# Decode rows of the row-wise projections: one pass of matmuls behind the second half of the contraction, instead of one pass behind each half

## The reference

```python
# GLA (layers 0 and 3): v has 1024 columns
q, k, v, g, a = _split(h @ w_in, [GLA_KEY_DIM, GLA_KEY_DIM, GLA_VAL_DIM, GLA_VAL_DIM, GLA_GATE_RANK])
# DSA (layer 1): k has 1024 columns; it is also an output (k_rows_prompt, k_rows_sample)
q, k, v, g, iq, ik, iw = _split(h @ w_in, [DSA_WIDTH] * 4 + [IDX_HEADS * IDX_DIM, IDX_DIM, IDX_HEADS])
```

## Time and profile before

| | us |
|---|---|
| median of 3 runs | 1150.73 |
| lowest and highest run | 1149.67 and 1153.07 |
| span of the profiled execution | 1153.2 |

### The profile page before, as it was taken

One profiled execution on the slowest core, in us unless ns is written; L12 is line 12 of the kernel. 1 busy time (PEld: TensorE's weight loads), 2 busy tenths in 40 slices (PEclk: granted clock), 3 DMA queues, 4 the chain that ended last, 5 costly groups with the idle time before them and its releaser, 6 DMA issues. The chain is left out here.

```text
span 1153.2 us, 25599 instructions
## 1 busy us (share of the span) xinstructions
PE 1115.8 (97%) x10579; PEld 976.9 (85%) x10579; DVE 674.4 (58%) x1215; ACT 494.4 (43%) x968; POOL 382.5 (33%) x321
## 2 busy tenths in 40 slices
PE   8999999899999999999999999999999999999897
PEld 6889888799758988888955599999999889888796
DVE  6462255764999779776444555595444362255742
ACT  6542466643443322222254554322453451467643
POOL 5534313234313423114300044353344245312230
PEclk9999999999999999999999999999999999999999
DMA  5235233333314787884779932233220335233202
GB/s 174 96 110 165 87 116 111 129 82 100 112 56 151 237 280 237 273 308 138 256 285 409 377 116 91 66 101 127 83 74 3 111 107 163 78 128 111 97 33 78
DMA packets 127788, 168.81 MB, mean 146 GB/s; under 512 B 20385, under 2 KB 93481, under 8 KB 127664
## 3 DMA queue, kind: packets, MB, share of 16 engines
q1 hardware_dynamic: 115609, 152.59, 39.6%
q10 hardware_dynamic: 12062, 14.59, 3.6%
HBM read 150.70 MB, written 16.81 MB: 145 GB/s over the span
## 5 line engine op out<-in xcount | busy, mean ns | idle before, releaser
L737 POOL TENSOR_TENSOR w_lo<-raw,w_hi 128x512 fp32r<-128x512 f32 (+2 forms) x267 | 359.9, 1380 | 691.4 <-ACT w_hi L1501 691.4
L773 PE MATMUL psum<-h_hi,w_hi 128*128 128x272 f32 x1616 | 471.2, 292 | 6.6 <-DVE h_lo L2425 4.7
L775 PE MATMUL psum<-h_hi,w_lo 128*128 128x272 f32 x1616 | 467.3, 289 | 0.0
L774 PE MATMUL psum<-h_lo,w_hi 128*128 128x272 f32 x1616 | 464.9, 288 | 0.0
L773 PEld LDWEIGHTS psum<-h_hi,w_hi 128*128 128x128 f32 x1616 | 303.3, 188 | 20.2 <-issue 15.3
L774 PEld LDWEIGHTS psum<-h_lo,w_hi 128*128 128x128 f32 x1616 | 303.7, 188 | 0.1
L775 PEld LDWEIGHTS psum<-h_hi,w_lo 128*128 128x128 f32 x1616 | 303.0, 187 | 0.0
L1501 ACT ACTIVATE w_hi<-raw 128x1024 fp32r<-128x1024 f32 (+1 forms) x137 | 135.5, 1034 | 118.5 <-PE psum L775 81.0
L773 PE MATMUL psum<-w_hi,h_hi 128*128 128x512 f32 (+2 forms) x352 | 125.6, 357 | 1.4 <-DVE dsa_score_s L2519 0.8
L775 PE MATMUL psum<-w_hi,h_lo 128*128 128x512 f32 (+2 forms) x352 | 122.5, 348 | 2.3 <-issue 2.3
L774 PE MATMUL psum<-w_lo,h_hi 128*128 128x512 f32 (+2 forms) x352 | 122.5, 348 | 0.7 <-issue 0.7
(11 more groups left out here) (331 smaller groups left out, 1367.3 us busy)
## 6 DMA issues: line engine op xcount, KB each, us to landing
smp_keys<-in_cache_k_dram SPq DMA_DIRECT2D x128, 256.0 KB, 4.7
raw<-in_gla_w_in_dram SPq DMA_DIRECT2D x23, 1024.0 KB, 5.3
raw<-in_dsa_w_in_dram SPq DMA_DIRECT2D x17, 1024.0 KB, 5.3
spare<-in_cache_v_dram SPq DMA_DIRECT2D x34, 512.0 KB, 8.3
raw<-in_cache_v_dram SPq DMA_DIRECT2D x30, 512.0 KB, 8.6
gla_s_in<-in_state_gla_dram SPq DMA_DIRECT2D x16, 512.0 KB, 7.8
raw<-in_gla_w_out_dram SPq DMA_DIRECT2D x8, 1024.0 KB, 6.7
out_dram<-gla_s_in ACTq DMA_DIRECT2D x16, 512.0 KB, 4.6
```

What stands on the lines that cost most here:

```text
L737: pool.tensor_tensor(copies(key, pair_view(w_lo, key)[:, k]), raw_copies(key, k), copies(key, pair_view(w_hi, key)[:, k].bitcast(F32)), AL ...
L773: pe.matmul(out, lh, rh, start=start, stop=False)
L774: pe.matmul(out, lh, rl, start=False, stop=False)
L775: return pe.matmul(out, ll, rh, start=False, stop=stop)
```

## The change

The decode rows leave the loop over the halves. The prompt tiles run through both halves first; then the decode tile claims its bank and runs all eight channel tiles in one go, the first four from the raw buffer of the first half and the last four from that of the second. The signal `("item", key)` is now raised by the last prompt tile of a half, and a new signal `("raw", key)`, for both halves, by the last decode matmul. SyncE's loads into these buffers wait for the new signal, and so would GpSimd's use of a raw buffer at L709. Matmuls, operands and their number stay.

```diff
@@ SyncE, -550,7 @@
                     elif s < RAW and by_rows(old):
-                        sp.wait_ge(*on("proj", ("item", old)))
+                        sp.wait_ge(*on("proj", ("raw", old)))
@@ GpSimd, -706,7 @@
                         if by_rows(bands_after):
-                            pool.wait_ge(*on("proj", ("item", bands_after)))
+                            pool.wait_ge(*on("proj", ("raw", bands_after)))
@@ t_job, -888,20 +888,12 @@
-                    for t in range(TILES):
+                    for t in range(NP_T):
                         if before_tile:
                             before_tile(x, t)
                         if x == 0:
                             bs.append(claim(next_bank(banks), ("proj", name, t), (reader_name, name, t)))
                         for k in range(kk):
-                            if t == SMP:
-                                if k0 + k == 0:
-                                    pe.wait_ge(*(on("h_s", name[0]) if name[0] else on("h_s", 0, SMP, 0)))
-                                for j in range(4):
-                                    mm = pe.matmul(psum[band(j), bs[t], 0:P], h_s[:, k0 + k, :],
-                                                   raw_view(key)[:, k, j * P:(j + 1) * P],
-                                                   start=k0 + k == 0, stop=k0 + k == KT - 1)
-                                continue
                             if t == 0:
                                 split_in(key, k)
@@ -909,12 +901,23 @@
-                        last_t = ((("item", key),),) if t == TILES - 1 else ()
+                        last_t = ((("item", key),),) if t == NP_T - 1 else ()
                         if x == len(keys) - 1:
                             mm.then_inc(*sig("proj", (name, t), also=last_t))
-                        elif t == TILES - 1:
+                        elif t == NP_T - 1:
                             mm.then_inc(*sig("proj", ("item", key)))
+                    if before_tile:
+                        before_tile(x, SMP)
                     k0 += kk
+
+                b = claim(next_bank(banks), ("proj", name, SMP), (reader_name, name, SMP))
+                pe.wait_ge(*(on("h_s", name[0]) if name[0] else on("h_s", 0, SMP, 0)))
+                for k in range(KT):
+                    w = raw_view(keys[k // 4])[:, k % 4]
+                    for j in range(4):
+                        mm = pe.matmul(psum[band(j), b, 0:P], h_s[:, k, :], w[:, j * P:(j + 1) * P],
+                                       start=k == 0, stop=k == KT - 1)
+                mm.then_inc(*sig("proj", (name, SMP), also=tuple((("raw", key),) for key in keys)))
```

## The result

The changed kernel takes 1154.58 us (median of 20 runs, 1151.32 to 1157.33) where the kernel before, run beside it, takes 1152.22 (20 runs, 1149.67 to 1155.03). The ratio is 1.0023, with a 95% interval of 1.0013 to 1.0033: 2.6 us slower (0.0023 x 1152.22; the medians are 2.4 us apart), less than 0.3% but clear of the scatter. The forecast of 1151.2 us was 0.5 us above the median then shown; the sign of its sum was right, the size was not, and the measured time lies just above the range (1154.4).

A forecast was written before the change was run, and what follows sets the result against it. The tensor engine, busy 97% of 1153.2 us, was taken as the bound. Merging -2.3, key block 0 stall +2.3, last layer's value block 1 +0.5 gave +0.5 us on the 1150.73 median: 1151.2 us, range 1148.4 to 1154.4.

The forecast's parts named there:

- The gain from merging: Decode passes (L901), 12 merged into 6: six entries and exits of 0.38 us go, 2.3 us gained (1.9 at least).
- The stop: Sparse layer, behind key block 0: late load holds ScalarE, tensor engine waits for third old-key tile, 2.3 us (1.7 to 2.6).
- rival B: Clock falls behind the new idle stretch in key block 0, costing 1.7 us: 1152.9 us; chance 0.20.
- Value blocks 1: Late low halves stall the tensor engine: last layer 0.5 us (0.4 to 1.3), first layer nothing if the clock falls again.
- What I costed at nothing: Late loads behind sparse key block 1, page loads and gated layers' k 1: hidden; otherwise 1 to 2 us a place.
- The sum: Whole kernel: -2.3 + 2.3 + 0.5 + 0, a difference of +0.5 us, giving 1151.2 us; ends -0.2 to +2.0.
- C: Key block 0's load lands after 7.9 us: stall 4.7 us plus a clock drop of 1.7, 1155.3 us; chance 0.12.
- A: Late loads are hidden after all, including ScalarE's stop in key block 0: 1148.4 us; chance 0.12.
- D: Merged passes save nothing, entering and leaving costs as much per half as before; only losses stay: 1153.5 us; chance 0.08.

The follow-up runs named there:

- changed, again: The changed kernel repeated unchanged, beside two other runs on one chip: 1153.41 us, ratio 1.0019 to the kernel before.
- held buffers only: The kernel before with its twelve passes, only the release of both raw buffers moved to the end of the block: 1155.82 us, ratio 1.0043.
- no stores: The changed kernel without ScalarE's five stores of block 0's key rows in the sparse layer and the wait for them: 1153.66 us, ratio 1.0012.
- q 0 held back: The changed kernel with SyncE's load of q 0 held until key block 1's first half is done: 1153.45 us, ratio 1.0013.
- the one with the split moved: The changed kernel with ScalarE's split of key block 1's second half behind all eight old-key tiles: 1150.73 us, 0.9990; again 1150.79 us, 0.9986.
- the kernel with key block 0 in halves: The changed kernel with the sparse layer's key block 0 alone in its old form, pass and buffer release per half: 1151.18 us, ratio 1.0000.

## Why the prediction was wrong, step by step

The stretch behind key block 0 in all the traces that have the stop, below a first row without it. "Third tile" is the start of its matmul, counted from the end of the block; "stretch" runs to the key transposes.

| kernel | load landed after | third tile | stretch | clock behind it |
|---|---|---|---|---|
| before | early enough | 6.1 | 14.46 | full |
| changed | 6.8 | 9.5 | 20.50 | half |
| changed, again | 5.6 | 8.3 | 16.70 | full |
| held buffers only | 6.4 | 9.1 | 17.47 | full |
| no stores | 5.2 | 7.9 | 17.71 | half, for a shorter time |
| q 0 held back | 5.1 | 7.8 | 16.18 | full |

- **The gain from merging.** 0.38 us a block predicted, 0.34 measured, 2.0 us in place of 2.3. The mechanism was right. The edges went as the sum had it; the 32 records that a pass gained took 1.89 - 1.01 = 0.88 us, where 32 steps of 0.026 are 0.84, and that is the missing 0.04.
- **The stop.** Place, chain and formula held: landing + 0.13 + 0.07 - 3.24 - 0.2 gives 2.4 us for 5.6 and 3.6 for 6.8, and the third tile came 2.2 and 3.4 us late. What was too narrow is the bound on the landing. I took 4.9 to 5.8 us, its lower part from the value blocks of the other layers, and put 7.9 aside as an outlier of one; in the ten traces with the load held back behind key block 0 it took 5.1 to 6.8, 5.7 on average. At 5.7 the stop is 2.5 us, close to the 2.3 of the sum, and up to 3.4 happens.
- **The clock.** This is the step that failed. I had it as rival B with a chance of 0.20 and 1.7 us, and outside the sum. Among the five traces with a stop and nothing to fill it, it fell in two, once behind 3.4 us and once behind 2.15, and not behind 2.95, 2.2 and 1.7. It cost 2.7 us in the first (the two steps of 2.93 and 2.94 in place of 1.61) and 1.5 in the second, so (2.7 + 1.5) / 5 = 0.8 us on average of the five. The ratios leave some more: from the changed kernel (1.0023 and 1.0019) to the one with the split moved (0.9990 and 0.9986) it is 0.0033, 3.8 us, and less the 2.5 of the stop 1.3 us. Both are estimates: the first rests on five executions, the second on ratios whose intervals reach about 0.001 to either side. How often the clock falls behind the stop stays open. The mean granted clocks fit but do not decide: the changed kernel has 0.9948, the kernel before on the three chips used behind it 0.9961 to 0.9968, but side by side on one chip they are 0.9957 and 0.9961, and the kernel with key block 0 in halves, which has no stop, has 0.9958. The price of a fall was sized from the first layer, 4 us at 0.66 and 0.50; the half clock lasted longer in the profiled execution.
- **Value blocks 1.** Last layer: 0.5 us predicted. From the block's start to the fifth slice it took 3.50 us (921.38 to 924.88) and was 2.88 (a slice of three products is 0.70, four of them and the entry), so 0.6. First layer: nothing predicted, as the clock would fall there again. It stayed up in this execution, and the place took 3.63 us, 0.7 more than at full clock and less than the 4.45 of the profile before, as the text had it. In the fourteen traces the clock fell here in eight, so the 0.7 counts in some executions and not in others.

```profile
919.05 4.99 POOL L737 TENSOR_TENSOR w_lo<-raw,w_hi 128x512 fp32r<-128x512 f32 x4 [15.09 <-ACT w_hi L1504]
921.38 0.50 PE L773 MATMUL psum<-w_hi,h_hi 128*128 128x512 f32 x1
...
924.09 0.50 PE L773 MATMUL psum<-w_hi,h_hi 128*128 128x512 f32 x1 [0.27 <-POOL w_lo L737]
```

- **What I costed at nothing.** It held: behind key block 1 ScalarE was idle 3.92 us on the load of q 1 and began the split at 372.52, GpSimd at 373.66, and no wait of the tensor engine for it shows. No wait for k 1 of the gated layers shows either, and the waits at the page loads are no longer than before (2.0 us in place of 2.3 at the value pages).
- **The sum.** With what was measured: -2.0 for merging, +2.5 for the stop at the average landing, +0.6 and up to +0.7 for the value blocks, +0.8 to +1.3 for the clock, together +1.9 to +3.1 us; the ratio says +2.6. Three small errors went the same way, 0.3 + 0.2 + up to 0.8, and the clock was left out.
- **The rivals.** What happened is B in part of the executions, and most of C in the profiled one: the landing was 6.8 where C has 7.9, the stop 3.4 where it has 4.7, the clock fell. A is out by the stop in every trace of the changed kernel, D by the 1.89 us of the merged pass (it wanted over 2.1).

The price of a clock that falls belonged into the sum as soon as the change made a new idle stretch beside an old one, with the chance as its weight. I gave it a chance, but then let the likeliest single case stand for the whole. My own 0.20 x 1.7 would have added only 0.3 us, so the chance and the price were too low as well.

That the measured 1154.58 lies above the range has a second cause, which is no part of the mechanism. The kernel before was itself measured 1.5 us higher with twenty runs than with the three that were shown, and the end of the range was 3.2 us above the forecast. Of the 3.4 us between forecast and measurement, 1.5 are this base, and 1.9 are what the change cost beyond the 0.5 of the sum; on the base that was shown, the same loss of 2.4 us between the medians would have ended at 1153.1, inside the range.

The Trainium skill, "TensorE: Matmul & The Clock Gate", section "What's actually happening", has the moment at which the clock changes vary from run to run of one and the same kernel. The two profiled executions of the changed kernel agree: half clock behind the stop in one, full clock in the other.

## What to carry to other kernels

When a buffer is held longer, look for the engine that waits for the late load and then for what stands behind that wait in its program: here the load landed at 323.9 us and the tensor engine came to the first product with it only at 353.8, but the copy behind it was needed at once. Moving the early split behind the urgent copies cost nothing that shows and turned a loss of 0.2% into a gain of about 0.1%, as far as that can be measured. A new idle stretch on the tensor engine has two prices, its length and, in some executions, a slower clock behind it; the second was 2.7 us beside a stop of 3.4 in one execution and nothing in others.

## What the runs showed of the hardware

- A stretch in which the tensor engine stood still for 1.3 to 1.8 us and then, some 3 us later, for 1.7 to 3.4 us was followed by the half clock in two of five traces, for up to 6 us; a stop of 2.95 us had a full clock behind it, one of 2.15 (and 1.33 before it) hadn't. The same program differed by 5.9 us in its span between two executions, 3.8 of them in this stretch (20.50 against 16.70).
- A load of 1 MB that was first in its queue landed after 4.9 to 5.4 us behind value block 0 of the first and last layer, but after 5.1 to 6.8 us behind key block 0 and after 5.4 to 8.2 behind key block 1. The one behind it landed some 2.3 us later (9.1 against 6.8, issued 0.4 us later), the third of three after 9.5 to 11.3 in those value blocks.
- Leaving and entering a run of small float32 matmuls among fp32r products costs 0.34 us a time, as much as thirteen of the 0.026 us steps inside it.
